# Even and odd layers: projecting the raw residual times the norm's weights, with each token's norm factor applied afterwards

## The reference, cut to what matters

```python
def rmsnorm(x, g):
    y = x * lax.rsqrt(jnp.mean(x * x, axis=-1, keepdims=True) + 1e-6)
    return y * g

x = rms_norm(x + gt_f * ((silu(gate) * up) @ w_down), final_norm)      # end of the first block
for layer in range(2):
    h = rmsnorm(x, attn_norm[layer])
    if layer == 0:                                                    # even
        qa, ka, va, qb, kb, vb, qi, ki, wi = split_cols(h @ w_in_even, sizes_even)
        # o_a: causal softmax(qa ka^T / 8 + bias) va, 8 heads of 64
        # o_b: per query keep the 64 keys with the highest
        #      sum_h relu(qi_h . rmsnorm(ki, k_norm) / 8) * wi_h / 4 ; then softmax as above
    else:                                                             # odd
        qc, kc, vc = split_cols(h @ w_in_odd, sizes_odd)              # 16 heads, biased softmax
    x = x + mixed @ w_o[layer]
    h = rmsnorm(x, ffn_norm[layer])
    x = x + conv_ffn(h, w_up[layer], ..., w_down[layer])
return rmsnorm(x, final_norm_2)
```

## Time and profile before

| | |
|---|---|
| median of 3 runs | 1666.41 us (1663.88 to 1666.53) |
| the profiled execution's own time | 1664.79 us |
| its span, first to last instruction | 1663.0 us |
| granted TensorE clock, mean | 0.959 of full |
| TensorE busy | 1530.4 us, 92% |
| VectorE / ScalarE / GpSimd busy | 1011.4 / 809.6 / 228.8 us |

### The profile page before, as it was taken

One profiled execution on the slowest core, in us unless ns is written; L12 is line 12 of the kernel. 1 busy time (PEld: TensorE's weight loads), 2 busy tenths in 40 slices (PEclk: granted clock), 3 DMA queues, 4 the chain that ended last, 5 costly groups with the idle time before them and its releaser, 6 DMA issues.

```text
span 1663.0 us, 29667 instructions
## 1 busy us (share of the span) xinstructions
PE 1530.4 (92%) x12458; PEld 1458.6 (88%) x12458; DVE 1011.4 (61%) x1297; ACT 809.6 (49%) x1297; POOL 228.8 (14%) x94
## 2 busy tenths in 40 slices
PE   6999978899889899879999798879999999899997
PEld 3987878899889877879999798879999898799997
DVE  2775457876656744585544557757874545477843
ACT  3754354443347544544433345546754455456632
POOL 0002218534500022270000000100000001000000
PEclk8999998999999999989999899989999999899999
DMA  9445844645554365244444443344534543334441
GB/s 389 174 152 213 293 178 183 230 174 205 190 187 158 124 251 206 102 179 175 169 156 171 152 153 131 123 153 152 184 138 175 187 153 124 130 136 168 171 159 76
DMA packets 30336, 287.85 MB, mean 173 GB/s; under 512 B 2903, under 2 KB 11383, under 8 KB 11800
## 3 DMA queue, kind: packets, MB, share of 16 engines
q1 hardware_dynamic: 26968, 267.42, 43.4%
q0 software_dynamic: 1152, 16.78, 2.6%
q10 hardware_dynamic: 2112, 2.15, 0.4%
HBM read 285.23 MB, written 7.39 MB: 176 GB/s over the span
## 4 chain that ended last, share of the span: by engine, by line
PE 75%; DVE 8%; ACT 6%; issue 4%; DMA 3%; POOL 3%; SPq 0%; DVEq 0%; ACTq 0%; POOLq 0%
PE bank L635 21%; PE bank L636 21%; PE bank L637 21%; PE bank L707 2%; ACT w_hi L1367 2%; DVE w_lo L1851 2%; DMA ring<-w_out 2%; PE bank L941 1%; PE bank L772 1%; POOL arena L2441 1%; PE bank L785 1%; PE bank L731 1%; POOL arena L2439 1%; DMA arena<-ada 1%; PE bank L745 1%
## 5 line engine op out<-in xcount | busy, mean ns | idle before, releaser
L635 PE MATMUL bank<-hi_T,w_hi 128*128 128x256 f32 x2184 | 635.7, 291 | 39.5 <-DVE h_lo L1834 16.4
L1851 DVE TENSOR_TENSOR w_lo<-ring,w_hi 128x2048 fp32r<-128x2048 f32 (+1 forms) x226 | 522.0, 2319 | 180.8 <-ACT w_hi L1367 179.2
L637 PE MATMUL bank<-hi_T,w_lo 128*128 128x256 f32 x2184 | 629.0, 288 | 0.0
L636 PE MATMUL bank<-h_lo,w_hi 128*128 128x256 f32 x2056 | 593.5, 289 | 0.0
L1367 ACT ACTIVATE w_hi<-ring 128x2048 fp32r<-128x2048 f32 (+1 forms) x226 | 392.0, 1735 | 276.7 <-PE bank L637 268.4
L635 PEld LDWEIGHTS bank<-hi_T,w_hi 128*128 128x128 f32 x2184 | 431.7, 198 | 45.7 <-issue 29.3
L637 PEld LDWEIGHTS bank<-hi_T,w_lo 128*128 128x128 f32 x2184 | 431.3, 197 | 0.0
L636 PEld LDWEIGHTS bank<-h_lo,w_hi 128*128 128x128 f32 x2056 | 407.5, 198 | 0.1
L635 PE MATMUL bank<-act_hi,w_hi 128*128 128x256 f32 x704 | 201.5, 286 | 10.5 <-DVE act_lo L1870 9.0
L636 PE MATMUL bank<-act_lo,w_hi 128*128 128x256 f32 x704 | 200.6, 285 | 0.0
L637 PE MATMUL bank<-act_hi,w_lo 128*128 128x256 f32 x704 | 200.4, 285 | 0.0
(11 more groups left out here) (236 smaller groups left out, 1988.6 us busy)
## 6 DMA issues: line engine op xcount, KB each, us to landing
ring<-w_gu SPq DMA_DIRECT2D x22, 2048.0 KB, 7.8
ring<-w_dn SPq DMA_DIRECT2D x32, 1408.0 KB, 6.0
ring<-w_up SPq DMA_DIRECT2D x22, 2048.0 KB, 7.8
ring<-ada SPq DMA_DIRECT2D x16, 2048.0 KB, 9.0
ring<-w_mix SPq DMA_DIRECT2D x11, 2048.0 KB, 7.9
arena<-ada POOLq DMA_DIRECT2D x8, 2048.0 KB, 8.9
ring<-even_in SPq DMA_DIRECT2D x8, 2048.0 KB, 7.8
ring<-odd_in SPq DMA_DIRECT2D x6, 2048.0 KB, 7.7
```

The source lines that it names most:

```text
L635: nc.tensor.matmul(out, wh, xh, start=start, stop=False)
L636: nc.tensor.matmul(out, wh, xl, start=False, stop=False)
L637: return nc.tensor.matmul(out, wl, xh, start=False, stop=stop)
L1851: V.tensor_tensor(w_lo[:, n % SLOTS, at], ring[:, n % SLOTS, at], w_hi[:, u % AHEAD, 0:size].bitcast(F32), ALU.subtract).then_inc(w_lo_rea ...
```

## The change

Both norms are taken off the way between the down projection and the input projections that follow it. A norm's factor belongs to a token, and a projection is linear, so the projection is made of `x` times the norm's weights, and the factor goes to the results:

- As soon as `residual` has added tile k, VectorE makes `h` = x times the weights (`postponed`), ScalarE `hi_T` and the squares of tile k, VectorE `h_lo` (`postponed_low`). Behind `dn1` the weights are the product of `final_norm` and the even layer's (`both_gains`). The squares go to spare room in `mix`; VectorE adds up five of them (`add_squares`), behind `dn1` two rows of squares side by side, plain ones and ones weighted for the second norm.
- TensorE's `first_tiles` follows the last down tile, and behind it three products by ones (`sum_late_squares`) in place of the eight (twice eight behind `dn1`).
- Root and reciprocal follow while TensorE goes on (`late_root`, `late_norm`). `x` is scaled by `final_norm` there too, and two tiny products (`turn_rows`) turn the factor from a row into a column.
- The factor then goes to: the index key, the index `relu` (as its scale) and `wi`; to the keys, two tiles at a time (`scale_keys`, four times in each layer); to the logits as the scale of the query rows; to the values as the scale of the copy out of PSUM (`tokens_taken`). TensorE waits for the scaled keys by `k_scaled`.

```diff
@@ norms that keep the old way
+    late_norms = ("dn1", "down0")
+    own_gap = [n for n in range(len(norm_input)) if n not in (4, 5, 7)]
+        late_squares = mix[:, :, :].rearrange("p (a b) n -> p a (b n)", a=4)
+        SQ_SLOT = (0, 1, 2, 1, 2, 1, 3, 2)
...
@@ TensorE
+            def sum_late_squares(l):
+                w = (2 - l) * S
+                for slot, added, squares in ((0, 5, 0), (3, 0, 7), (2, 0, 8)):
...
+                    last = nc.tensor.matmul(bank[:, 6, 0:w], const("ones"), late_squares[:, slot, 0:w],
+                                            start=(slot == 0), stop=(slot == 2))
+            def turn_rows(l):
+                pe.wait_ge(row_ready, l + 1)
+                for qt in range(QT):
+                    last = nc.tensor.matmul(bank[:, 5, qt:qt + 1], rstd[0:1, qt * P:qt * P + P], const("ones")[0:1, 0:1],
+                                            start=True, stop=True)
...
                 half_in(h0)
-                taken(0)
                 first_tiles(split_half(h0, CH // 2), (hi_T, h_lo), normalised(first))
+                sum_late_squares(0)
                 columns_half(1, 2)
...
                 columns_half(4, 7)
+                turn_rows(0)
                 pe.wait_ge(ki_sq, 1)
...
+                pe.wait_ge(k_scaled, 2)
                 scores(u0)
...
-            norm_sums(n)
             n += 1
             for l, woven_layer in enumerate((even_layer, odd_layer)):
-                norm_sums(n)
                 woven_layer(norm_end[n] - KT)
@@ ScalarE
+            def squares_and_high(l, n):
+                u0 = phases[late_norms[l]]["u0"]
+                for k in range(KT):
+                    high(u0 + 2 * k + AHEAD)
+                    if k < KT - 1:
+                        high(u0 + 2 * k + 1 + AHEAD)
+                    act.wait_ge(hn_ready, KT * split_norms.index(n) + k + 1)
+                    nc.scalar.activation(hi_T[:, k, :], h[:, k, :], ACT.Copy).then_inc(h_hi_ready, 1)
...
+                    if l == 0:
+                        nc.scalar.activation(late_squares[:, at, S:2 * S], x[:, k, :], ACT.Square,
+                                             scale=const("final1")[:, k:k + 1])
+                    nc.scalar.activation(late_squares[:, at, 0:S], x[:, k, :], ACT.Square).then_inc(late_sq, 1)
+                high(u0 + 2 * KT - 1 + AHEAD)
+            def late_root(l):
+                act.wait_ge(late_ssq, l + 1)
+                nc.scalar.activation(std[:, :], bank[:, 6, 0:S], ACT.Sqrt, bias=const("eps"), scale=1.0 / D)\
+                    .then_inc(late_std, 1)
+                if l == 0:
+                    act.wait_ge(mean_ready, 1)
+                    nc.scalar.activation(std[:, :], sg[:, 0, :], ACT.Sqrt, bias=const("eps"), scale=1.0 / D)\
+                        .then_inc(late_std, 1)
...
                 two_taken("first", 0, h0, 0, (16, 17))
+                late_root(0)
                 two_taken("first", 2, h0 + 1, 0, (18, 19))
...
-            norm_squares(n)
...
-                norm_squares(n)
-                norm_high(n)
+                squares_and_high(l, n)
@@ VectorE
+            def postponed(k, gain):
+                V.tensor_scalar(h[:, k, :], x[:, k, :], gain[:, k:k + 1], None, ALU.mult).then_inc(hn_ready, 1)
+            def postponed_low(n, k):
+                dve.wait_ge(h_hi_ready, KT * split_norms.index(n) + k + 1)
+                V.tensor_tensor(h_lo[:, k, :], h[:, k, :], hi_T[:, k, :].bitcast(F32), ALU.subtract).then_inc(h_ready, 1)
+            def add_squares(l, k):
...
+                V.tensor_tensor(late_squares[:, 0, 0:w], late_squares[:, 0, 0:w], late_squares[:, SQ_SLOT[k], 0:w], ALU.add)\
+                    .then_inc(late_added, 1)
+            def scale_keys(t, name, tiles):
+                dve.wait_ge(gemm_freed, phases[name]["t0"] + tiles)
+                V.tensor_tensor(qk2[:, t:t + 2, :], qk2[:, t:t + 2, :], over(rstd[:, :], 2), ALU.mult).then_inc(k_scaled, 1)
+            def late_norm(l):
+                if l:
+                    dve.wait_ge(late_std, 3)
+                    V.reciprocal(rstd[:, :], std[:, :]).then_inc(row_ready, 1)
...
+                ch(V.reciprocal(r_first, std[:, :]))
+                ch(V.tensor_tensor(sg[:, 0, :], bank[:, 6, S:2 * S], r_first, ALU.mult))
+                V.tensor_tensor(sg[:, 0, :], sg[:, 0, :], r_first, ALU.mult).then_inc(mean_ready, 1)
+                low(phases["first"]["u0"] + AHEAD)
+                for k in range(KT):
+                    ch.mark(V.scalar_tensor_tensor(out=x[:, k, :], in0=x[:, k, :], scalar=const("final1")[:, k:k + 1],
+                                                   in1=r_first, op0=ALU.mult, op1=ALU.mult))
+                dve.wait_ge(late_std, 2)
+                ch(V.reciprocal(rstd[:, :], std[:, :]))
+                V.tensor_tensor(rstd[:, :], rstd[:, :], r_first, ALU.mult).then_inc(row_ready, 1)
...
@@ VectorE, in residual(name, gate, late)
                     ins.then_inc(gemm_freed, 1)
+                    if late:
+                        l, n, gain = late
+                        dve.wait_ge(gemm_freed, ph["t0"] + k + 1)
+                        postponed(k, gain)
+                        if k == KT - 1:
+                            postponed_low(n, k)
                     used = range(ph["u0"] + 2 * k, ph["u0"] + 2 * k + 2) if each == 2 else [ph["u0"] + k // 2] * (k % 2)
                     for u in used:
                         if u < ph["u1"] - 1:
                             low(u + AHEAD)
+                    if late and k < KT - 1:
+                        postponed_low(n, k)
+                        if 1 <= k <= 5:
+                            add_squares(l, k)
...
-            normalise_into(n, const("final1"), x, x_ready)
...
-                normalise(n, vec_b(l, "norm_attn"))
```

More of the change, by code:

```diff
@@ L478, in biased_units @@
                              for s, r in ((t, LO), (t + 2, HI))] for t in range(2)],
-                        start=True, end=True, qs=qs, mix_at=2 * (g0 + g)))
+                        start=True, end=True, qs=qs, mix_at=2 * (g0 + g), row_scale=r_scale[:, qt:qt + 1]))
             return us
@@ L1192, in even_layer @@
                 taken(21)
+                pe.wait_ge(k_scaled, 3)
                 scores(u0 + 2)
@@ L1203, in even_layer @@
                 taken(25)
+                pe.wait_ge(k_scaled, 4)
                 scores(u0 + 4)
@@ L1261, in odd_layer @@
                 taken(10)
+                pe.wait_ge(k_scaled, 7)
                 scores(u0 + 2)
@@ L1267, in odd_layer @@
                 taken(14)
+                pe.wait_ge(k_scaled, 8)
                 scores(u0 + 4)
@@ L1276, in odd_layer @@
                 taken(18)
+                pe.wait_ge(k_scaled, 9)
                 scores(u0 + 6)
@@ new lines, in scale_keys, with late_columns @@
+            def scale_keys(t, name, tiles):
+                dve.wait_ge(gemm_freed, phases[name]["t0"] + tiles)
+                V.tensor_tensor(qk2[:, t:t + 2, :], qk2[:, t:t + 2, :], over(rstd[:, :], 2), ALU.mult).then_inc(k_scaled, 1)
+            def late_columns(l):
+                dve.wait_ge(rows_turned, l + 1)
+                ch(V.tensor_copy(r_column, bank[:, 5, 0:QT]))
+                ch(V.tensor_scalar(r_scale, r_column, SCALE, None, ALU.mult))
+                if l == 0:
+                    for qt in range(QT):
+                        last = V.tensor_scalar(wi[:, qt, :], wi[:, qt, :], r_column[:, qt:qt + 1], 16 ** -0.5,
+                                               ALU.mult, ALU.mult)
+                        ch.mark(last)
+                    ch.wait()
+                V.tensor_copy(r_column, r_column).then_inc(column_ready, 1)
@@ L2121, in residual @@
+            def residual(name, gate, late=None):
                 ph = phases[name]
@@ L2270, in even_layer @@
                 index_sums(5)
+                scale_keys(4, "even", 8)
                 low(h0 + 9 + AHEAD)
@@ L2283, in even_layer @@
                 recip(u0 + 1)
+                scale_keys(6, "even", 14)
                 low(h0 + 12 + AHEAD)
@@ L2293, in even_layer @@
                 recip(u0 + 3)
+                scale_keys(12, "even", 18)
                 low(h0 + 14 + AHEAD)
@@ L2305, in even_layer @@
                 evac(u0 + 4)
+                scale_keys(14, "even", 24)
                 low(h0 + 17 + AHEAD)
@@ L2333, in odd_layer @@
                 evac(u0)
+                scale_keys(6, "odd", 10)
                 low(h0 + 6 + AHEAD)
@@ L2339, in odd_layer @@
                 recip(u0 + 2)
+                scale_keys(10, "odd", 14)
                 low(h0 + 8 + AHEAD)
@@ L2346, in odd_layer @@
                 recip(u0 + 4)
+                scale_keys(14, "odd", 18)
                 low(h0 + 10 + AHEAD)
```

87 lines of the change are left out of this document (64 added, 23 removed).

## The result

| | before | changed |
|---|---|---|
| median of the runs, us | 1665.38 (4 runs, 1663.88 to 1666.53) | 1642.44 (4 runs, 1640.06 to 1645.18) |
| ratio to before, 95% interval | | 0.9864 (0.9842 to 0.9887) |
| profiled execution: span, us | 1663.0 | 1643.4 |

The changed kernel is faster by 1.36%. The forecast was 1642, with a range from 1638 to 1649.

What follows compares the result with a forecast made beforehand. TensorE, busy 92% of 1663.0 us, was taken as the bound, so time is won where it waits or runs slowly. 16.8 + 8.0 - 1.0 - 0.1 = 23.7 us off 1664.79, plus 1.6 for the median, gave 1642, range 1638 to 1649.

Steps and rivals of the forecast that it cites:

- First hole: TensorE's gap behind `dn1`, ahead of the even layer: 25.15 us shrink to 8.35, so 16.8 us won.
- Second hole: TensorE's gap behind `down0`, where one norm lies: 15.0 us shrink to 7.05, so 8.0 us won.
- The operands are there: At the first tiles: tile 7's operands need about 2 us, TensorE wants them after 5.0, cover 3 us.
- Full clock for the first tiles: Behind the down tiles, the 48 products run 0.12 us apart, 5.76 us, as the slow start goes with the hole.
- the 4.8 us "in either hole" of the rival: First tiles stay at 0.22 us a product, 10.6 us not 5.76; time 1652; chance placed with a partly open hole, 0.06.
- Down tiles keep 7.92 us: Down projection: VectorE's 5.1 us and ScalarE's 4.0 us a tile fit under TensorE's 7.92, so added work costs nothing.
- the point of decision: Rival that VectorE and ScalarE bind the down tiles: slower from 9.4 us a tile, 1674 at 10 us; chance 0.02.
- `turn_rows`, 0.5 us each: In each woven layer, four one-column records on TensorE's path cost 0.5 us.
- `scale_keys`, 0.1 us for all: Woven layers: eight VectorE key scalings of 0.69 us, 5.5 us if none were hidden, cost 0.1 us together.
- Scales that are columns, nothing: In relu, logits and value copies, column scales replace constants: counted nothing; 3 us busy time if 32 took 0.1 more each.
- slow stretch gone: In the tail's narrow products behind the first hole, the low clock goes too, 2.75 us lost before; time 1639; chance 0.09.
- Given back: In the woven layers, key scalings, `k_scaled` waits and wider scales lie on the path; 1645 to 1649 us; chance 0.13.

Runs made afterwards that it cites:

- the even layer alone: Against the kernel before, only the norms behind `dn1` are postponed and the odd layer stays as before; 1650.46 us, ratio 0.9903.
- the odd layer alone: Against the kernel before, only the norm behind `down0` is postponed and the even layer stays as before; 1659.46 us, ratio 0.9965.
- the run that used it up: Changed kernel plus idle VectorE work ahead of the last down tile's multiplication, 2.3 us in `dn1`, 4.6 in `down0`; second hole's stretch 70.34 us, against 68.46.
- the tiles loaded: Changed kernel plus idle VectorE work ahead of `h_lo` in each down tile but the last; `dn1` stretch 58.42 us, `down0` stretch 74.03.

## Why the prediction was right, point by point

- **First hole, 16.8 us.** Right: 75.26 - 58.41 = 16.85 in the kernel with the even layer alone, 16.8 to 17.1 in the others. The tiles take 5.76 us as said, the sums 2.57 (921.22 to the slot ahead of 923.91). The stretch with the old hole took 76.66 us in the kernel with the odd layer alone, 1.4 more than before, so this term is good to about that.
- **Second hole, 8.0 us.** Right: 76.44 - 68.46 = 7.98.
- **The operands are there, cover 3 us.** Right: 3.05 by the rows of the last tile of `dn1`, 3.04 behind `down0` by the run that used it up.
- **Full clock for the first tiles.** Right: 48 products 0.12 us apart, where before they began 0.22 apart. The Trainium skill (TensorE: Matmul & The Clock Gate, section "HAM oscillation — how this bites in real kernels") states that the burst behind a long wait starts at half rate; by that rule the trace agrees behind `dn1`, where the 0.22 went with the wait, and doesn't behind `down0`. There the old kernel had the same wait of 4.09 us, and its first products stood 0.12 us apart; the distance grew to 0.21 only from 1323.11 on:

```profile
1322.16 0.28 PE L636 MATMUL bank<-h_lo,w_hi 128*128 128x256 f32 x1
1322.28 0.28 PE L637 MATMUL bank<-hi_T,w_lo 128*128 128x256 f32 x1
...
1323.11 0.41 PE L635 MATMUL bank<-hi_T,w_hi 128*128 128x256 f32 x1
1323.32 0.41 PE L636 MATMUL bank<-h_lo,w_hi 128*128 128x256 f32 x1
```

  So the 4.8 us "in either hole" of the rival rested on a row of the first hole only.
- **Down tiles keep 7.92 us.** Right, and tried: 2.3 us more on VectorE in each tile of `dn1` cost nothing, and in `down0` the point of decision is some 3.4 us.
- **`turn_rows`, 0.5 us each.** A little short. Copies 119 to 120, between which the first stands, take 6.91 us instead of 6.18; copies 176 to 178, around the second, 13.18 instead of 12.56: 0.73 and 0.62, together 1.35 instead of 1.0. From the slot behind the last product (948.86 + 0.12) to the next product's start at 949.60 it is 0.62 us, not 4 x 0.12; the recorded bound, nothing to twice 0.5, holds.
- **`scale_keys`, 0.1 us for all.** Short by 0.3 at least: 0.4 us in the odd layer, and in the even one some 0.4 in one step that the sum of the layer doesn't show. The reason given was only half of it. At the place that the prediction called the tightest it came out well: TensorE waits there for the last scaling of the even layer (0.62 us, which the view puts down to "issue"; without the scalings there is no wait at these scores), and smaller waits of 0.30 and 0.25 us right behind it are gone in return, while the one for `mix_lo` is 2.84 us and was 2.78:

```profile
1060.47 0.71 PE L775 MATMUL bank<-arena 64*128 64x128 f32 x8 [0.62 <-issue]
```

  But the prediction looked at VectorE and TensorE only, and where a scaling does cost time it is by GpSimd's step, which is slower beside it.
- **Scales that are columns, nothing.** A copy of values of 512 columns takes ScalarE 0.69 us where it took 0.60, what the estimate allowed, and there may be 0.25 us on the path: six steps between copies 120 and 137 are 0.05 to 0.1 us longer or shorter in the kernels with the new even layer, by 0.25 together. (This is argued from the distances; no run had the scales as constants.) The stretch is longer by 0.5 to 1.5 us in six profiles with the new even layer and the narrow tail against the two with the old one. The rest, up to 1.2 us, lies in the steps 126 to 127 and 129 to 130, at the same share of low clock before and after; some 0.4 us of it goes with the scalings, and what is left stays open.
- **The tail.** The rival "slow stretch gone" was wrong, and the forecast that it stays was right: 5 us lost in the changed kernel's profile, 3.4 in its repetition, 3.4 before, and 1.7 with the tiles loaded. That it would cost the same before and after is true only within this spread.

Sum of what was measured: 16.85 + 7.98 - 1.35 - 0.4 - 0.25 = 22.8 us. With the whole lengthening of the even layer, 0.5 to 1.5 us, and another 0.16 in the odd one it is 21.4 to 22.4. The medians show 22.9. The forecast had 23.7 by the same terms. The medians can't decide among these: by the interval of the ratio the gain is 18.8 to 26.3 us. That 1642.44 lies within half a us of the forecast is therefore luck; what is shown is that the two holes and their terms were right.

"Given back" was 0.65 us of key scalings and column scales, and some 2 us at most with all that is open in both layers, less than the 2.75 to 6.5 of the rival. The single profile, with 19.6 us between the spans, would have misled here: of the 3.3 us by which it falls short of the medians 1.7 stand in the tail (2.43 less 0.73 for `turn_rows`), where two runs of the same kernel differ by 1.75.

## What to carry to other kernels

A factor that belongs to a token alone commutes with the projection, so a norm's sums, root and reciprocal can be taken off the path: start the products on what is there, and apply the factor to the results, on engines that idle. What it is worth is read from the two edges of the hole, less the work that remains in it; whether it can be had is one figure, the cover of the last operand, here 3 us of 5. And each new wait on such a factor should stand on the helping engine ahead of work that nobody waits for: one line moved there took 2.4 us off a wait and 1.7 us off its step. Look also at what the third engine does at that moment: a scaling beside GpSimd's step made that step 0.36 us longer.

## What the runs showed that I had not expected

- TensorE busy 100% of a stretch and yet at 0.50 of its clock: in the changed kernel the clock falls behind 24 products of 16 columns and stays low over 935 to 945 us; the same work as 256-column products ran at 1.00 throughout the tail. How long the fall lasts differs between profiles with the same tail (0.50, 0.50, 1.00 or 0.66, 0.78, 0.88 over three stretches), so the same tail takes from 18.6 to 21.8 us.
- GpSimd's multiplication takes 1.40 us instead of 1.04 when a VectorE multiplication of 512 columns runs beside it, in every profile with that order; without the scaling it is 1.04.
- Lateness on a helping engine is not paid tile by tile: 1.19 us more in each of seven tiles cost 5.6 us, not 8.3, since a lead of 3 us had to be used up first.
